# A streaming encoder layer on one core: who issues the projections' stores, and how the expert work is dealt out beside each kind of step

## The reference, cut to what matters

```python
n = rms_norm(x)
fq, fk, fv, ff, sq, sk, sv, ga, gb = split(n @ w_in)          # 3 x 512, 8, 3 x 512, 1024, 1024
h = x + (sigmoid(ga) * (fox(fq, fk, fv, ff) @ w_o_fox)
         + sigmoid(gb) * (stick_breaking(sq, sk, sv) @ w_o_sb)) @ w_out
out = h + peer(rms_norm(h))

def peer(x):                                                   # 128 experts of 16384 for every row
    eidx, g = product_key_top16_of_each_of_8_heads(x)
    act = gelu(einsum('thkd,td->thk', expert_u[eidx], x))
    return einsum('thk,thkd->td', g * act, expert_v[eidx])
```

## Time and profile before

| | |
|---|---|
| median of 3 runs | 4417.79 us (4407.78 to 4420.72) |
| the profiled execution's own time | 4408.68 us |
| its span, first to last instruction | 4406.9 us |
| granted TensorE clock, mean | 0.804 of full |
| PE busy | 3126.3 us (71%) |
| DVE busy | 2947.4 us (67%) |
| ACT busy | 1195.7 us (27%) |
| POOL busy | 1432.8 us (33%) |
| moved by DMA | 1415.74 MB, 321 GB/s over the span |

### The profile page before, as it was taken

One profiled execution on the slowest core, in us unless ns is written; L12 is line 12 of the kernel. 1 busy time (PEld: TensorE's weight loads), 2 busy tenths in 40 slices (PEclk: granted clock), 3 DMA queues, 4 the chain that ended last, 5 costly groups with the idle time before them and its releaser, 6 DMA issues. The chain is left out here.

```text
span 4406.9 us, 31690 instructions
## 1 busy us (share of the span) xinstructions
PE 3126.3 (71%) x9474; PEld 1614.2 (37%) x9474; DVE 2947.4 (67%) x5644; ACT 1195.7 (27%) x2527; POOL 1432.8 (33%) x1085
## 2 busy tenths in 40 slices
PE   8876689956557988837549898745486688845665
PEld 3353344533224544513225554412243343512222
DVE  1126465487768865897758864987575675897665
ACT  2211155101115651012126641111254451111110
POOL 0002222122433432333423332333232243345563
PEclk9788867987777889978868889877687789867777
DMA  5356978765998998978989888969876799979997
GB/s 169 99 204 259 347 292 319 278 248 211 412 377 345 389 380 325 370 276 328 410 322 362 343 338 324 369 255 398 315 300 262 279 366 346 402 301 369 420 420 321
DMA packets 325161, 1415.74 MB, mean 321 GB/s; under 512 B 37368, under 2 KB 105248, under 8 KB 178528
## 3 DMA queue, kind: packets, MB, share of 16 engines
q0 software_dynamic: 154464, 1116.02, 63.6%
q1 hardware_dynamic: 170528, 297.70, 19.4%
HBM read 1377.95 MB, written 35.10 MB: 321 GB/s over the span
## 5 line engine op out<-in xcount | busy, mean ns | idle before, releaser
L662 POOL DMA_INDIRECT uv<-expert_uv,rows_u x1024 | 1376.5, 1344 | 2542.4 <-PE pv L758 1310.9
L758 PE MATMUL pv<-uv,diag 128*128 128x512 f32 x2052 | 1153.0, 719 | 511.6 <-ACT diag L1057 472.6
L1288 DVE CUSTOM_DVE_ANT_0 uv<-uv,nr 128x1024 f32<-128x1024 f32 x1056 | 1238.5, 1219 | 153.1 <-DMA uv<-expert_uv,rows_u 118.7
L926 PE MATMUL pb<-arena 128*128 128x512 f32 (+1 forms) x1440 | 703.1, 646 | 278.1 <-DMA arena<-w_main 278.1
L758 PEld LDWEIGHTS pv<-uv,diag 128*128 128x128 f32 x2052 | 462.0, 235 | 1116.9 <-issue 1074.8
L1314 DVE SCALAR_TENSOR_TENSOR held<-uv,wgt,held 128x1024 f32<-128x1024 f32 x542 | 696.5, 1285 | 19.2 <-DVE wgt L1299 0.3
L1064 ACT ACTIVATE gel<-dots 128x4 f32<-128x4 f32 x264 | 54.2, 205 | 1841.3 <-DVE dots L1288 1770.1
L926 PEld LDWEIGHTS pb<-arena 128*128 128x128 f32 (+1 forms) x1440 | 280.4, 201 | 667.3 <-issue 369.2
L711 PE MATMUL pb<-arena 64*128 64x512 f32 (+6 forms) x544 | 284.3, 638 | 164.0 <-DVE arena L1270 46.6
L1299 DVE TENSOR_TENSOR wgt<-gel,gw 128x4 f32<-128x4 f32 x256 | 41.8, 163 | 350.2 <-ACT gel L1064 350.2
L740 PE MATMUL pb<-arena 128*128 128x64 f32 (+3 forms) x1728 | 248.4, 291 | 33.4 <-ACT o L1046 28.3
(11 more groups left out here) (144 smaller groups left out, 2515.4 us busy)
## 6 DMA issues: line engine op xcount, KB each, us to landing
arena<-w_main SPq DMA_DIRECT2D x100, 1024.0 KB, 13.0
arena<-w_stream SPq DMA_DIRECT2D x80, 1024.0 KB, 7.2
uv<-expert_uv,rows_u POOLq DMA_INDIRECT x1024, 10.3
arena<-x SPq DMA_DIRECT2D x16, 512.0 KB, 14.1
scratch_gates<-arena SPq DMA_DIRECT2D x32, 256.0 KB, 8.8
arena<-scratch_gates SPq DMA_DIRECT2D x8, 1024.0 KB, 17.1
arena<-scratch_c_p SPq DMA_DIRECT2D x8, 520.0 KB, 7.4
arena<-x_t SPq DMA_DIRECT2D x8, 512.0 KB, 4.4
```

Source lines behind the costliest of these rows:

```text
L662: pool.indirect_dma_start(out=uv[k % NU][:].rearrange("p a n -> p (a n)"), out_offset=None, in_=io["expert_uv"][:, :], in_offset=bass.Indi ...
L758: mm = nc.tensor.matmul(pv[:, c * BANK:(c + 1) * BANK], diag[n % ND][:], uv[k % NU][:, 1, c * BANK:(c + 1) * BANK], start=n == first, stop ...
L926: mm = nc.tensor.matmul(pb[0:r, proj.slot(c, ti), :], xt[:, half * 4 + f, ti * P:ti * P + r], w[:, f, :], start=half == 0 and f == 0, stop ...
L1288: nc.vector.tensor_tensor_reduce(out=u, in0=u, in1=row[:], scale=1.0, scalar=0.0, op0=ALU.mult, op1=ALU.add, accum_out=dots[b % 2][:, k % ...
```

## The change

Two parts.

**The stores.** `store_stage` and `store_turned` leave SP's program. ACT gets `store_column` and `store_turned`, with the same DMAs, after its own copies of the same column. `tst` grows from two buffers to four (`NT`), so that the copy waits for the store of four turns ago and not of two.

**The lots.** The weights of the steps are now one per kind (`SHARE`), and so is the number of a lot's four slots that DVE sums (`ON_VECTOR`); beside attend and at the end of the kernel the old alternation of one and two stays.

```diff
+NT = 4
-STEP_LOTS = 2.6
+SHARE = {"project": 1.9, "attend": 0.56, "outputs": 0.8, "y": 1.5, "merged": 0.8, "h": 1.5, "norm": 0.8, "turned": 0.8,
+         "queries": 1.0, "halves": 1.0, "experts": 0.8}
+ON_VECTOR = {"project": 4, "y": 4, "h": 4, "outputs": 2, "merged": 2, "norm": 2, "turned": 2, "queries": 2, "halves": 0, "experts": 0}
...
     def on_dve(self, k):
         j = k % NK
-        if self.step_of.get(k // LOT) == "project":
-            return True
+        kind = self.kind_of.get(k // LOT)
+        if kind in ON_VECTOR:
+            return j % LOT < ON_VECTOR[kind]
         return j % LOT == 0 or (j % LOT == 1 and j // LOT % 2 == 1)
...
-        tst = [carve(BANK) for _ in range(2)]
+        tst_more = [carve(BANK) for _ in range(2)]
...
+        tst = [carve(BANK) for _ in range(2)]
+        tst += tst_more
...
                         for n in (2 * c + NW, 2 * c + 1 + NW):
                             if n < 2 * COLS:
                                 load_half(g, n)
-                        store_stage(g, c)
-                        if c - 1 in QK:
-                            store_turned(g, c - 1)
...
-                        if n >= 2:
-                            act.wait_ge(t_stored[n % 2], proj.t_stored[n - 2])
+                        if n >= NT:
+                            act.wait_ge(t_stored[n % NT], proj.t_stored[n - NT])
...
+                    def store_column(c):
+
+                        for ti, t in enumerate(tiles):
+                            r, sem = rows_of(t), s_stored[proj.slot(c, ti)]
+                            row = stage[proj.slot(c, ti)]
+                            if c == 1:
+                                act.wait_ge(normed, proj.normed[g, c, ti])
+                                store_rows(act, (io["fk_p"], io["fk_s"]), row, t, sem)
...
+                            elif c >= 6:
+                                act.wait_ge(staged, proj.staged[g, c, ti])
+                                act.dma_start(dram["gates"][t * P:t * P + r, (c - 6) * BANK:(c - 5) * BANK], row[0:r]).then_inc(sem, 16)
+
+                    def store_turned(c):
+                        for ti, t in enumerate(tiles):
+                            n = proj.turned[g, c, ti]
+                            act.wait_ge(col_turned_out, n + 1)
+                            for r0, w, at in positions(t):
+                                act.dma_start(dram[SCRATCH[c]][:, at:at + w].rearrange("(g p) t -> p g t", p=P),
+                                              tst[n % NT].rearrange("p (g t) -> p g t", g=4)[:, :, r0:r0 + w]).then_inc(t_stored[n % NT], 16)
...
                         if c - 1 in QK and len(tiles) > 1:
                             turn_out_column(c - 1, 1)
+                        if c - 1 in QK:
+                            store_turned(c - 1)
+                        if c == 2:
+                            store_column(1)
+                        if c >= 2:
+                            store_column(c)
```

More of the change, by code:

```diff
@@ L119, in __init__ @@
         staged = normed = turned = 0
-        slots, banks = [0] * 4, [0] * 2
+        slots, banks = [0] * 4, [0] * NT
         for g, tiles in enumerate(NEW):
@@ L135, in __init__ @@
                     if c in QK:
-                        banks[turned % 2] += 16 * len(positions(t))
-                        self.t_stored[turned] = banks[turned % 2]
+                        banks[turned % NT] += 16 * len(positions(t))
+                        self.t_stored[turned] = banks[turned % NT]
                         self.turned[g, c, ti] = turned
@@ L216, in __init__ @@
         self.tiles = [sum(subs, ()) for subs in WAVES]
-        self.lots, self.step_of = {}, {}
+        self.lots, self.kind_of = {}, {}
         for g in range(1, len(WAVES)):
-            steps = [(("project", g, c), STEP_LOTS * len(NEW[g]) / 2) for c in range(COLS)]
-            steps += [(("attend", g, s), 1) for s in range(self.end[g] - self.first[g])]
-            steps += [(("merge", g, s), 1) for s in range(len(merge_steps(self.tiles[g])))]
+            steps = [(("project", g, c), "project", SHARE["project"] * len(NEW[g]) / 2) for c in range(COLS)]
+            steps += [(("attend", g, s), "attend", SHARE["attend"]) for s in range(self.end[g] - self.first[g])]
+            steps += [(("merge", g, s), name[0], SHARE[name[0]]) for s, name in enumerate(merge_steps(self.tiles[g]))]
             first, count = self.tiles[g - 1][0] * LOTS, len(self.tiles[g - 1]) * LOTS
-            total, done = sum(w for _, w in steps), 0
-            for i, (step, w) in enumerate(steps):
+            total, done = sum(w for _, _, w in steps), 0
+            for step, kind, w in steps:
                 a = first + int(done * count / total + 1e-6)
@@ L228, in __init__ @@
                 for b in self.lots[step]:
-                    self.step_of[b] = step[0]
+                    self.kind_of[b] = kind
         self.rest = range(self.tiles[-1][0] * LOTS, ALL_SLOTS // LOT)
@@ L363, in stream @@
         at[0] = project_end
+        tst = [carve(BANK) for _ in range(2)]
+        tst += tst_more
+        assert at[0] <= ARENA - KINDS * (KS + 10 * PW + 2 * P)
         ls, cs = carve(KS)[0:HEADS], carve(KS)[0:HEADS]
@@ L383, in stream @@
         s_stored = [sem(f"s_stored{i}") for i in range(4)]
-        t_stored = [sem(f"t_stored{i}") for i in range(2)]
+        t_stored = [sem(f"t_stored{i}") for i in range(NT)]
         v_stored, c_stored = sem("v_stored"), sem("c_stored")
@@ L541, in load_rows @@
                         sp.dma_start(xr[ti][0:r], io["x"][t * P:t * P + r, :]).then_inc(xr_in[ti], 16)
[L543 to L564, removed]
                 def store_forget(g):
@@ L602, in project @@
                         if c == 7 and g:
-                            for i in range(2):
+                            for i in range(NT):
                                 sp.wait_ge(t_stored[i], proj.all_t[g][i])
```

6 lines of the change are left out of this document (5 added, 1 removed).

## The result

The changed kernel takes 4374.4 us (median of 4 runs, 4370.35 to 4381.61), against 4417.8 before; the ratio is 0.9916, with a 95% interval of 0.9893 to 0.9938, so some 37 us. The forecast was a gain of 99 us. The sign was right, the size less than half.

A forecast was written before the change was run, and what follows sets the result against it. Attend was taken as bound by engine work, project by bytes, merge by PE and DVE. Attend -116, project -20, merge +42, stores -5 made -99: 4310 us from the profiled 4408.7, 4319 as median; range 4250 to 4400.

The forecast's parts named there:

- Attend, -116: Attend, four waves: 22 lots fewer, at 5.1 us each in waves 1 to 3 and 5.6 in wave 4.
- Rival 1: DVE sets the pace of attend, which then gives -158: 4277 us; chance 0.13.
- Project, -20: Project of waves 2 and 3: bound by bytes, one lot fewer in each saves 10.1 us.
- Outputs to turned, +55: First part of merge: added lots turn its bound from PE to memory; 0, +21, +21, +13 us by wave.
- Queries, +40: Queries part of merge: added lots' bytes cost 0, +5, +5 and +30 us by wave.
- Halves and experts, -53: Last part of merge: DVE's sums go to PE, one lot more from wave 2; -10.3, -13, -13, -17 us.
- Stores, -5: Stores moved from SP to ACT: -5 us at the start and drain of project, between 0 and -75.
- rival 4: The store waits are paid back in full, PE gets weights in time: -75 us, 4249 us; chance 0.10.
- Rivals 3: Stores block ACT before gelus, four waves at 38 us, +150: 4469 us, slower; chance 0.07.
- Rival 2: 18 added lots in merge, waves 2 to 4, cost 10.1 us each: 4406 us; chance 0.15, shared with another rival.

The follow-up runs named there:

- e5: The changed kernel with the old numbers of lots per step, keeping the new split and the stores on ACT: 4346.6 us, ratio 0.9854 to the kernel before.
- e10: The changed kernel with every gather fetching only the u half, half the bytes, all engines doing the same instructions: 4009.3 us, one run.
- e1: The changed kernel with the old lots and old split, so only the stores move to ACT, with four tst buffers: 4400.4 us, ratio 0.9983.
- e6: The changed kernel with the new numbers of lots but the old split of sums between DVE and PE: 4418.2 us, ratio 1.0022.
- e9: e8 with the old numbers of lots per stage: 4277.0 us, ratio 0.9688 to the kernel before.
- e8: e7 plus the attention's first pair load issued one column later, behind the last half of the weights: 4308.9 us, ratio 0.9768.
- e7: The changed kernel with no lots at second y, second h and norm, their weight moved to outputs, first y, merged and turned: 4338.2 us, ratio 0.9843.
- e12: e1 with two tst buffers instead of four: 4364.8 us, one run.

## Why the prediction was right and wrong, point by point

- **Attend, -116: right in the sum, in part by luck.** It was -117.3 in the changed kernel and -117.5 between e5 and it, and in waves 1 to 3 bytes don't move it (271 us in wave 2 of e10). By waves it was -6, -27, -31 and -53 against -15, -31, -31 and -39: a lot was worth 2 us in wave 1 and 7.5 in wave 4. Of wave 4's 53 us, 17 are shorter waits of PE for the loads (82.8 us before, 66.2 after), which the price of a lot didn't hold and which differ by up to 30 us between kernels with equal lots. Rival 1 falls.
- **Project, -20: wrong; this is the first step that failed.** "Bytes set this stage" is true (e10), but the lot taken away had not been in the stage: 72 dots before and after. The term of the lots' bytes had to be 0 in these two waves, and was (-1 us from e1 to e6). What the prediction put at nothing was the split: it adds 13 us to the projects with the old numbers and 25 with the new ones. Stores, numbers and split together are -13, -10 and +25, the +2 of the changed kernel against a forecast of -25.
- **Outputs to turned, +55, measured +70: the second, and in its mechanism the main failure.** "This part changes its bound from PE to memory" was wrong. In wave 2 the bytes gave 137 us and 133.7 were measured, but half the bytes give 133.7 too (e10). The sentence that DVE's 101 us of work are "still inside 116" was the step: busy time was summed, and the work was not followed through the engines in its order. The lots at y and h are done by DVE and ACT in series with the merge's own rows, so that PE's waits for them grew, and PE was idle 47 us of this part in wave 2 instead of 20. Waves 1 and 4, where bytes gave 0 and +13, got +11 and +26. That the added lots cost 70 us, 5.4 each, is measured for both orders (e5 to the changed kernel, e9 to e8), and 76 us with the old split (e1 to e6). How it divides among DVE, ACT and PE was not tested; an estimate of the four dots of a lot on DVE, 4 x 1.22 = 4.9 us, is near it. The place of the lots among the steps, 44 to 46 us (e7, and e9 against e5), is a cost beside this one. With it mended and the new numbers, waves 2 to 4 ran at 404 to 420 GB/s, where bytes may take over.
- **Queries, +40, measured +44: right in size, not in cause.** e10 leaves 92.1 us in waves 2 and 3, and in wave 4 takes 6 of the 31 away. That work paces these steps is argued, from PE's 87 of 92 us in wave 2 and DVE's 98 of 109 in wave 4; no run takes it apart.
- **Halves and experts, -53, measured -37: right mechanism, a term mis-sized.** The split alone gave -54 (e1 to e5), where 8 + 14 + 14 + 17 sums were priced at 68. In wave 2 the sums in this window fell from 15 to 2 and not from 14 to none, since two of the last lot of queries still fall in it. The lot more cost 16 against 15, though 3.5 of it came in wave 1, which got none. DVE was busy 139 us in wave 2 and not under 130. (The prediction counts 20 PE slots more in wave 2; by the plan they are 18.)
- **Stores, -5**: -7 with an interval of +2 to -17. Of the copies' waits, which rival 4 wanted paid back, e12 brings 27 us back and the projects stay as they are. Rivals 3 and 4 fall: ACT's issues were as long as 12.7 us, but DVE's wait for gelus didn't grow (352 us before, 284 in e1). The Trainium skill (DMA: Bandwidth & Descriptors, "Issuing engines are not separate DMA queues") says that issuing from another engine saves only the sequencer's issue time. The prediction made 0 of it for this term, and the measurement holds both 0 and -5.
- **Rival 2** (the added lots have no cover) wanted 182 us for the 18 lots of outputs to turned and queries in waves 2 to 4; they cost 105, the forecast had 95. Only wave 4's queries had its size, 31 us for three lots. Its cause, weights and gathers colliding, is refuted by e10 for waves 1 to 3, and in wave 4's queries half the bytes take back only 6 of the 31.
- The sum: -99 forecast, -36 in the span. Of the 63 between them, 27 are project, 15 outputs to turned, 4 queries, 16 halves and experts.

What stays open: why the v loads of wave 4 land late in some kernels, what the 5.4 us of an added lot in outputs to turned consist of, and whether the 126.5 us of e7 in wave 2 are a floor of bytes (half the bytes were not tried there).

## What to carry to other kernels

When background work is moved between stages, price it at both ends in the order of each in-order engine, not by busy sums or by bytes alone: ask which result of the foreground is next in that engine's program behind the moved work, and put the work where nothing is. A stage at the plateau of memory isn't therefore bound by it; halving the bytes of the background and leaving every instruction in place tells it in one run. And before crediting a stage with work taken away, count in the trace whether that work ran there.

## What the runs showed of the hardware

- In outputs to turned of wave 2 the mean granted clock was 0.86 before, where PE was idle 19.5 of 117.6 us, and 0.77 after, where it was idle 47.2 of 133.7. PE's busy time fell by 11.6 us, where an estimate by seven slots of 2.14 us gives 15.
- With memory at the plateau an issue can hold its engine for long, on ACT's queue as on SP's: two v loads took 19.0 us to issue on SP, two stores 8.4 us on ACT. It need not: two stores took 1.0 us on ACT just before those, and 0.9 us on SP in a slice of 388 GB/s. What decides between the two is not shown.
- With rows of 4 KB instead of 8 the tail of 40 lots ran in 316 us, 7.9 us a lot, at 281 GB/s in its middle. There DVE is busy for 185 of 200 us, so its work is likely the next bound behind the bytes.
